# Gate projections of a hybrid recurrent layer as 24 problems of seven block products, with the block sums on GpSimd

## What is computed

```python
z = h @ p['w_in']                       # h: 1056 x 1024 (modulated RMSNorm)
u_a, p_b, q_c, f_c, i_c, og_c, gate_logits = jnp.split(z, IN_SPLITS, axis=-1)
...                                     # S5 branch y_a, RWKV-7 branch y_b, HGRN2 branch y_c
gates = jax.nn.sigmoid(gate_logits).reshape(n, l, N_BRANCH, D_MODEL)     # 3 x 1024 columns
merged = (gates[:, :, 0] * (y_a @ p['w_lift_a'])
          + gates[:, :, 1] * (y_b @ p['w_lift_b'])
          + gates[:, :, 2] * (y_c @ p['w_lift_c']))
h_res = h_res + gt1[:, None, :] * (merged @ p['w_out'])
```

## Time and profile before

| | us |
|---|---|
| median of 3 runs | 2179.43 (2177.44 to 2182.61) |
| the profiled execution, whole | 2179.46 |
| its span (first to last instruction) | 2177.5 |
| HGRN2 part, about | 238 to 398 |
| RWKV-7 part, about (j = 0, 1, 2, 3) | 421 to 1124 |
| lifts and merge from | 1124 |
| feed-forward part from | about 1400 |

### The profile page before, as it was taken

One profiled execution on the slowest core, in us unless ns is written; L12 is line 12 of the kernel. 1 busy time (PEld: TensorE's weight loads), 2 busy tenths in 40 slices (PEclk: granted clock), 3 DMA queues, 4 the chain that ended last, 5 costly groups with the idle time before them and its releaser, 6 DMA issues.

```text
span 2177.5 us, 43013 instructions
## 1 busy us (share of the span) xinstructions
PE 2121.5 (97%) x18759; PEld 1581.0 (73%) x18759; DVE 1170.3 (54%) x1763; ACT 475.1 (22%) x900; POOL 395.3 (18%) x419
## 2 busy tenths in 40 slices
PE   6999999999999999999999998999999999999999
PEld 4666666666667667666666687888888888888887
DVE  5777344162353353334334656777773366777645
ACT  3122121232132142142110003122220022333001
POOL 2520000001002002001100000745500345544000
PEclk8999999999999999999999999999999999999999
DMA  8310132301112111120236322111013411111302
GB/s 315 109 44 11 58 127 96 97 5 59 51 49 60 46 56 45 46 72 27 79 132 208 118 80 79 40 41 41 26 60 114 138 40 41 41 42 38 130 30 80
DMA packets 123173, 161.59 MB, mean 74 GB/s; under 512 B 22108, under 2 KB 93057, under 8 KB 122971
## 3 DMA queue, kind: packets, MB, share of 16 engines
q1 hardware_dynamic: 101568, 132.68, 18.8%
q10 hardware_dynamic: 21420, 26.17, 3.3%
HBM read 126.24 MB, written 32.59 MB: 73 GB/s over the span
## 4 chain that ended last, share of the span: by engine, by line
PE 95%; DVE 2%; issue 1%; SPq 1%; ACT 1%; DMA 1%; ACTq 0%; DVEq 0%
PE ps L1018 94%; PE ps L1022 1%; SPq L633 1%; DVE hT L2648 0%; DVE arena L2648 0%; ACT hT L2455 0%; DVE Y L2648 0%; DMA arena<-in_state_s_dram 0%; SPq L650 0%; DMA hT<-gates 0%; ACT arena L2122 0%; DVE arena L2880 0%; SPq L654 0%; DVE W L2648 0%; ACT arena L2433 0%
## 5 line engine op out<-in xcount | busy, mean ns | idle before, releaser
L1018 PE MATMUL ps<-hT,W 128*128 128x352 f32 (+1 forms) x3272 | 951.9, 443 | 9.6 <-DVE hT L2773 4.7
L1018 PEld LDWEIGHTS ps<-hT,W 128*128 128x128 f32 x3272 | 613.5, 191 | 272.1 <-issue 24.5
L1018 PE MATMUL ps<-arena 64*64 64x64 f32 (+7 forms) x9264 | 461.0, 248 | 18.2 <-issue 15.9
L1018 PEld LDWEIGHTS ps<-arena 64*64 64x64 f32 (+3 forms) x9264 | 361.5, 139 | 134.9 <-issue 75.9
L1018 PE MATMUL ps<-arena,W 128*128 128x264 f32 x1056 | 247.1, 386 | 0.0
L1018 PEld LDWEIGHTS ps<-arena,W 128*128 128x128 f32 x1056 | 200.6, 190 | 34.4
L878 POOL TENSOR_TENSOR arena<-arena,mixer 128x512 f32<-128x512 f32 x40 | 50.7, 1276 | 875.2 <-DVE flag L3119 763.3
L2648 DVE TENSOR_TENSOR Y<-Y,ps 128x528 f32<-128x528 f32 (+1 forms) x158 | 94.8, 600 | 163.2 <-PE ps L1018 150.3
L2648 DVE TENSOR_TENSOR arena<-arena 128x1056 f32<-128x1056 f32 (+6 forms) x162 | 141.9, 876 | 58.0 <-PE ps L1018 43.7
L2122 ACT ACTIVATE arena<-ps 128x512 f32<-128x512 f32 (+6 forms) x154 | 89.1, 588 | 371.8 <-PE ps L1018 279.1
L2122 ACT ACTIVATE Y<-ps 128x264 f32<-128x264 f32 (+1 forms) x92 | 43.0, 468 | 557.7 <-PE ps L1018 501.1
(11 more groups left out here) (329 smaller groups left out, 1795.4 us busy)
## 6 DMA issues: line engine op xcount, KB each, us to landing
W<-in_w_up_dram SPq DMA_DIRECT2D x22, 1024.0 KB, 6.7
W<-in_w_ada_dram SPq DMA_DIRECT2D x8, 2048.0 KB, 10.5
W<-in_w_in_dram SPq DMA_DIRECT2D x13, 1024.0 KB, 7.1
gates<-arena ACTq DMA_DIRECT2D x72, 176.0 KB, 1.9
arena<-xres SPq DMA_DIRECT2D x22, 528.0 KB, 4.8
arena<-gates SPq DMA_DIRECT2D x21, 528.0 KB, 3.7
xres<-arena ACTq DMA_DIRECT2D x16, 528.0 KB, 5.0
W<-in_w_ada_dram SPq DMA_DIRECT2D x32, 256.0 KB, 2.7
```

Source lines behind the costliest of these rows:

```text
L1018: return nc.tensor.matmul(out, lhsT, rhs, start=start, stop=stop, skip_group_check=True)
```

## The change

The gate projection is done as 24 problems. Problem p covers 256 output rows (chunk p % 12) and one half of the columns (528). Each is a product of a 2 x 2 block matrix of weights (blocks of 512 x 128) with a 2 x 2 block matrix of inputs (blocks of 512 rows by 264 columns), done with seven block products instead of eight, of four matmuls over 264 columns each: 672 matmuls in all. Each weight chunk is loaded twice, once for each half.

The operands of the seven need sums. POOL makes them: T1, T2, T3, T4 of the inputs once for each half (128 x 1056 each; T4 a second time for problems 20 to 23), and for each problem S1 and S3 (128 x 512, by `s1_s3`), S2 (in two halves of 256, `s2`), S4 (`s4`). ACT copies each of the seven products from PSUM (`save`, 128 x 264), and POOL adds three of them (`c11`, `c22`, `c12`, 128 x 264); the other sums are made by letting a bank go on accumulating after it was copied. Then `gates_out(p)` on ACT runs two sigmoids over 128 x 528 and stores each. `gate_steps(n)` on PE issues the next n of the 28 matmuls of a problem, wherever filling stood before.

```diff
+            def gate_steps(n):
+                for _ in range(n):
...
+                    b = 6 + (PRODUCTS * p + i) % 2
...
+                    lhs, rhs = ((A11, B11), (A12, B21), (A11, T2_), (gate_s1, T1_), (A21, T3_), (A11, B22), (A22, T4_))[i]
+                    if k == 0:
+                        take(b)
...
+                        elif i == 2:
+                            pe.wait_ge(sem("gate_sums"), 5 * p + 3)
...
+                        elif i == 5:
+                            pe.wait_ge(sem("gate_sums"), 5 * p + 5)
...
+                    elif i == 2 and k == 2:
+                        pe.wait_ge(sem("gate_sums"), 5 * p + 4)
+                    m = mm(pb[b][:, 0:HG], lhs[:, k, :], rhs[:, k, :], k == 0 and i in (0, 1, 3), k == 3)
```

```diff
+            def save(n=1):
...
+                    act.wait_ge(sem("gemm_done"), gate_product(p, i))
+                    if p and i in (0, 3):
+                        act.wait_ge(sem(f"ring_stored{i // 3}"), 16 * p)
+                    if p and i == 1:
+                        act.wait_ge(sem("gate_adds"), 3 * p)
+                    if i == 5:
+                        act.wait_ge(sem("gate_adds"), 3 * p + 1)
+                    if i == 6:
+                        act.wait_ge(sem("gate_adds"), 3 * p + 2)
...
+            def gates_out(p):
+                for a in range(2):
+                    rows_ = Z[0][:, HT * a:HT * (a + 1)]
+                    act.wait_ge(sem("gate_adds"), 3 * p + 3)
...
+                    nc.scalar.activation(rows_, rows_, ACT.Sigmoid).then_inc(sem("gate_out"), 1)
```

```diff
+            def whole_problem(p):
+                s2(p)
+                c11(p)
+                s4(p)
+                c22(p)
+                c12(p)
+                s1_s3(p + 1)
```

In the HGRN2 part the filling is dealt anew, and `outputs(t)` becomes two parts: `outputs_within` (which needs no states) and `outputs_carried` (which waits for `hg_states`), with filling between them:

```diff
                 for l in range(LEVELS):
-                    gate(12 * t + l)
+                    gate_steps((9, 11, 8, 10, 10, 8)[l])
                     level(t, l)
...
-                gate(12 * t + 6)
+                gate_steps(8)
                 updates(t)
-                gate(12 * t + 7, 12 * t + 8)
-                outputs(t)
-                gate(12 * t + 9)
+                gate_steps(9)
+                outputs_within(t)
+                gate_steps(10)
+                outputs_carried(t)
+                gate_steps(9)
                 head_sums(t)
-                gate(12 * t + 10, 12 * t + 11)
+                gate_steps(20)
```

412 lines of the change are left out of this document (272 added, 140 removed).

## The result

| | before | after |
|---|---|---|
| median, us (19 executions each) | 2182.82 (2177.44 to 2185.71) | 2170.15 (2161.46 to 2180.1) |
| profiled execution, us | 2179.46 | 2177.94 |
| its span, us | 2177.5 | 2176.0 |
| mean granted clock in it | 0.993 | 0.989 |

The ratio is 0.9946, interval 0.9935 to 0.9958: the change gains 0.54%, some 12 us. I had said 29.5 us and a range of 2137 to 2169, so the direction was right and the time lies just above the range. The times of the 19 executions go with the clock (2161.46 us at a mean clock of 0.995, 2180.1 us at 0.987), which is a first hint.

What follows compares the result with a forecast made beforehand. PE was taken as the bound (busy 97% of the span). Matmul savings of -42.0 us, plus entries, new waits and port, summed to -29.6 us from 2179.46: 2150 us predicted, range 2137 to 2169.

Steps and rivals of the forecast that it cites:

- The matmuls: Gate matmuls on PE: 576 x 0.592 us become 672 x 0.445, -42.0 us; six more groups of filling, +1.2 us.
- New wait 1: HGRN2's last filling: ACT's copy of product 1 waits for a store, PE for the bank; +1.0 us, twice, +2.0.
- the weights: Gate weight loads: 1 MB lands in 7.1 us, each place free a whole problem (12.5 us) ahead; priced at nothing.
- Rival D: Slower: ACT's line frees banks late, PE stands still once per problem; 2 us each gives 2198 us. Chance 0.07.
- rival C: Thinner filling or PE waiting halves the clock at each of 6 places: 6 x 1.45 = +8.7 us, 2159. Chance 0.08.
- New wait 2: HGRN2's last filling: `root` between copies delays product 6 by 0.9 us, twice, +1.8; `ada_cols(5)` behind sigmoids, +0.9.
- New wait 3: RWKV-7: `ada_rows` in bank 7 right after product 7 of the second problem; +0.2 us, four times, +0.8.
- New wait 4: End of RWKV-7: PE's state turning and lifts wait on ACT's line and the gates read back; +3.7 us, bounds 0 and 7.
- The port: DVE and POOL hold each other up in HGRN2's scalings, the mixes and decode: +2 us, bounds 0 and 12.
- sums: POOL's sums within and across gate problems are ready before PE needs them; priced at nothing.
- `LT`: POOL's `LT` shares its line with the sums but is released 7 us before it is needed; priced at nothing.

Runs made afterwards that it cites:

- e7_pieces: Changed kernel with second staging buffer, ACT's root earlier, and the 1 MB weight load of each j's third gate problem cut in four: 2154.28 us, ratio 0.988.
- e1_load_waits: Changed kernel, but SP issues the 1 MB weight load of problem p + 2 only after both stores of problem p have landed: 2170.49 us, ratio 0.9926.
- e2_second_buffer: Changed kernel with a second staging buffer for the gates of odd problems up to 15: 2158.9 us, ratio 0.9879.
- e5_tiny_sums: Changed kernel with nearly all of POOL's sums for the gates cut to 8 columns, most gates left uncomputed: 2171.1 us, ratio 0.9952.
- e12_lift_late: e7_pieces with the load of the second half of the lift weights (2 MB) moved behind the first six reads of the gates: 2152.34 us, ratio 0.9859.
- e13_shift64: e12_lift_late with 32 more 64x64 matmuls at the start of RWKV-7 with j = 0, which change nothing: 2150.77 us, ratio 0.9857.

## Why the prediction was right or wrong

- **The matmuls**, -42.0 and +1.2 us: nearly right. Four matmuls of 264 take 1.78 us from start to start, 0.445 each, and the ledger gives 35.5 to 39.1 us for 40.8.

```profile
266.60 1.94 PE L1158 MATMUL ps<-arena 128*128 128x264 f32 x8
...
268.38 1.94 PE L1158 MATMUL ps<-arena,W 128*128 128x264 f32 x8
```

- **New wait 1**, the step that failed. I took the landing of the store from the earlier trace rows (1.9 us for 176 KB, so 2.3 for 264), and asked only in the last filling of HGRN2 who waits for it. For a store alone 2.3 us was right (2.03 measured). At seven borders it is 6.0 to 6.3 us, since there the last matmul of a problem also frees the weights and starts a 1 MB load one us ahead of the store. I had priced the weights at nothing, looking only at when they arrive and not at what they do to the transfers beside them. And the wait is at every border of two problems at which little else stands: 2.64, 2.67, 1.82, 1.69 and 1.66 us, 10.5 us that my sum did not have. In the last filling, where I did look, PE waited 3.0 us for the 2.0 forecast, but only in part for my reason: the wait for the store came once (1.25 us with t = 0) and not twice. The 1.06 and 0.70 us stand one product earlier. There ACT copied the last product of the problem before only behind the four stores of the states, which I had in ACT's line without a price for PE. So this item came near its number partly by luck. The change itself made the dependence on the store: before, three buffers of 352 columns lay between a store and its next use.
- **Rival D** had this mechanism, with a wait of 2 us in each of 24 problems. It came in 5, at 1.7 to 2.7 us, and once with 1.25 us. My argument against it, that the branch's matmuls stand between two problems, holds for nearly all the others. I should have looked at each border instead of setting one price for all.
- **The clock**, rival C, was the second failure: I gave it 0.08 and treated it as a case of its own. The ledger has 15.4 us of it after, 3.4 before: +12.0 us in the profiled execution. It is no rival but an addition to some of the waits. The low windows of the changed kernel all stand at or behind a wait of PE (2.64, 2.67, 1.98, 1.54, 1.16, 2.36 and 3.22 us), but behind others the clock stayed up (1.82, 1.69 and 1.66 us here, 3.46 us in e7_pieces). With the waits for the store gone (e1_load_waits, e2_second_buffer) HGRN2 has no drop, so the waits play a part; but in e5_tiny_sums the first of them stood with 2.54 us and no drop behind it. What decides from one wait to the next stays open.
- **New wait 2**: 0.71 us twice for 0.9, and 1.06 for 0.9 ahead of `ada_cols(5)`. Right. **New wait 3**: no wait ahead of `ada_rows`, for 0.8 us in all, and one of 0.43 us ahead of `ada_cols` with j = 3. In its bounds.
- **New wait 4**, the end of RWKV-7: 1.41 + 0.55 + 3.22 - 0.38 = 4.8 us for 3.7, in its bounds. My working had a slip: from 14 to 19.4 us it is 5.4 us at the upper end and not 4.9. The last store took 5.75 us beside 2 MB of lift weights, which I had not priced here either. The lift behind it then took 6.67 us for 12 records of 352 columns instead of 3.79, at half clock, 2.9 us that I had not counted.
- **The port**: 1.3 us for 2, and e5_tiny_sums puts all of POOL's cost inside the error of the measurement. Right, as are the steps "sums" and "`LT`": PE waits for no sum.
- **Waits without a cause**: 14.4 us before, 19.3 after. They stood in the trace of before, and I did not ask what sets them. They depend on which matmuls the borders of 256 records fall on and on the loads in flight, and the change moves both.

Sum by the ledger: -40.8 + (20.5 + 5.1 - 3.1 - 1.8) + (19.3 - 14.4) + 12.0 = -3.2 us for the profiled pair, which differs by -1.5. The median shows more gain (12 us). Its mean clock is 0.991 where the profiled execution has 0.989; that the rest of the difference is the clock and the waits without a cause is argued from the spread, not shown for each execution.

With a second buffer, a load in pieces and the lift load moved (e12_lift_late, or with the shift e13_shift64) the kernel takes 2151 us, ratio 0.986. That is near what I had predicted for the change as it stood, but it took other edits to get there, and it confirms the matmul term and not my price for the waits.

## What to carry to other kernels

When a change gives a transfer someone who waits for it, price its landing beside the transfers that the same event releases, and ask at each place where it occurs what work lies between. Price a long wait of the tensor engine with a slow stretch that may follow it, and not alone: of the 36 waits of 2 us or more in these traces, 25 had a granted clock below 0.9 at the wait or in the 6 us behind it. Keep large loads away from dense runs of small matmuls. And when time appears or vanishes in dense runs of small matmuls, count instructions from wait to wait before looking for a cause in the change.
